# Shifting the low weight parts of a feed-forward by feature tile: 64, 192, 320 and 448 bytes in place of 64

## What is computed

```python
def swiglu(x, wi, wo):
    gate, up = jnp.split(x @ wi, 2, axis=-1)
    return (jax.nn.silu(gate) * up) @ wo
# per layer, D_MODEL = 1024, D_FF = 2816, SEQ = 256
h = h + 0.5 * swiglu(rmsnorm(h, ln_ffn1[i]), ffn1_wi[i], ffn1_wo[i])
h = h + mixer(rmsnorm(h, ln_mix[i]))
h = h + 0.5 * swiglu(rmsnorm(h, ln_ffn2[i]), ffn2_wi[i], ffn2_wo[i])
```

## Time and profile before

| | before |
|---|---|
| runs, median (lowest to highest) | 1936.55 us (1936.25 to 1936.56) |
| the profiled execution | 1937.1 us |
| its span, first to last instruction | 1935.4 us |
| PE busy | 1914.7 us, 99% of the span |
| PEld (weight loads) busy | 1653.1 us, 85% |
| DVE busy | 1366.3 us, 71% |
| ACT busy | 1128.9 us, 58% |
| chain that ended last, by engine | PE 93%, DVE 4%, ACT 2% |
| chain, by line | L698 33%, L535 31%, L706 17%, L993 5% |
| mean granted TensorE clock | 0.998 |

### The profile page before, as it was taken

The page is one execution under the profiler, slowest core; times in us unless marked ns, Lnnn a source line. Parts: engine busy times, 40 slices in busy tenths (PEclk is TensorE's granted clock), DMA queues, the critical chain, the costliest instruction groups (busy, mean ns, idle before and its releaser), DMA issues.

```text
span 1935.4 us, 29477 instructions
## 1 busy us (share of the span) xinstructions
PE 1914.7 (99%) x10740; PEld 1653.1 (85%) x10740; DVE 1366.3 (71%) x1844; ACT 1128.9 (58%) x1678; POOL 70.0 (4%) x151
## 2 busy tenths in 40 slices
PE   8999999999999999999999999999999999999998
PEld 6888988888888888888888889888888888978887
DVE  6766775777776697776776676676677777667666
ACT  6555575555655567655565555665555556656553
POOL 2000000000000002000010001000000000000000
PEclk9999999999999999999999999999999999999999
DMA  6556534655455554555655544355556555535553
GB/s 219 196 189 202 174 128 135 216 191 187 166 195 193 177 188 161 172 193 186 209 174 195 195 157 132 125 178 190 195 176 209 188 187 174 174 125 165 189 194 120
DMA packets 245264, 344.41 MB, mean 178 GB/s; under 512 B 12214, under 2 KB 197195, under 8 KB 245195
## 3 DMA queue, kind: packets, MB, share of 16 engines
q1 hardware_dynamic: 242016, 340.29, 53.2%
q10 hardware_dynamic: 3178, 3.18, 0.6%
HBM read 341.32 MB, written 1.06 MB: 177 GB/s over the span
## 4 chain that ended last, share of the span: by engine, by line
PE 93%; DVE 4%; ACT 2%; issue 0%; DMA 0%; SPq 0%; ACTq 0%; POOL 0%; POOLq 0%; DVEq 0%
PE psum L698 33%; PE psum L535 31%; PE psum L706 17%; PE psum L993 5%; DVE wlo L497 1%; PE psum L1644 1%; PE psum L566 1%; PE psum L1035 1%; DVE mix L1459 1%; ACT whi L478 1%; PE psum L1701 0%; DVE mix L1184 0%; DMA raw<-in_ffn_wi 0%; PE psum L1046 0%; PE psum L1731 0%
## 5 line engine op out<-in xcount | busy, mean ns | idle before, releaser
L478 ACT ACTIVATE whi<-raw,gains 128x512 fp32r<-128x512 f32 (+2 forms) x876 | 557.1, 709 | 260.6 <-PE psum L706 195.6
L698 PE MATMUL psum<-xT,whi 128*128 128x512 f32 x2816 | 679.4, 393 | 1.9 <-DVE wlo L518 1.5
L497 DVE SCALAR_TENSOR_TENSOR wlo<-raw,gains,whi 128x512 fp32r<-128x512 f32 (+2 forms) x876 | 596.0, 742 | 55.7 <-ACT whi L478 55.7
L698 PEld LDWEIGHTS psum<-xT,whi 128*128 128x128 f32 x2816 | 522.8, 188 | 111.1 <-issue 4.4
L706 PEld LDWEIGHTS psum<-xT,wlo 128*128 128x128 f32 x2816 | 344.4, 189 | 6.8
L706 PE MATMUL psum<-xT,wlo 128*128 128x256 f32 x2816 | 346.4, 281 | 0.0
L814 DVE TENSOR_TENSOR gate_in_T<-psum,low 128x512 f32<-128x512 f32 x88 | 60.8, 691 | 337.1 <-ACT low L761 336.7
L493 DVE TENSOR_TENSOR wlo<-raw,whi 128x2048 fp32r<-128x2048 f32 x100 | 228.5, 2285 | 43.4 <-ACT whi L474 43.4
L535 PE MATMUL psum<-whi,hidT_hi 128*128 128x512 f32 x640 | 249.0, 389 | 0.0
L535 PE MATMUL psum<-wlo,hidT_hi 128*128 128x512 f32 x640 | 249.0, 389 | 0.0
L535 PE MATMUL psum<-whi,hidT_lo 128*128 128x512 f32 x640 | 249.0, 389 | 0.0
(11 more groups left out here) (224 smaller groups left out, 1528.8 us busy)
## 6 DMA issues: line engine op xcount, KB each, us to landing
raw<-in_ffn_wi SPq DMA_DIRECT2D x350, 512.0 KB, 4.6
raw<-in_ffn_wo SPq DMA_DIRECT2D x176, 512.0 KB, 4.4
raw<-in_sb_w_in SPq DMA_DIRECT2D x48, 512.0 KB, 4.6
raw<-in_ml_w_in SPq DMA_DIRECT2D x24, 512.0 KB, 4.5
raw<-in_sb_w_out SPq DMA_DIRECT2D x16, 512.0 KB, 4.1
raw<-in_ml_w_out SPq DMA_DIRECT2D x8, 512.0 KB, 4.2
raw<-in_mla_w_out SPq DMA_DIRECT2D x8, 512.0 KB, 4.0
raw<-in_mla_w_in SPq DMA_DIRECT2D x4, 512.0 KB, 4.2
```

What stands on the lines that cost most here:

```text
L478: last = act.activation(whi[:, slot, r], raw[:, slot, r], ACT.Copy, scale=gain_col(p.gain + k))
L497: last = dve.scalar_tensor_tensor(wlo[:, slot, p.at + r.start:p.at + r.stop], raw[:, slot, r], gain_col(p.gain + k), hi[:, r], op0=ALU.mul ...
L698: i = pe.matmul(psum[:, 4 + blk, :], whi[:, slot, k * 2 * FC + blk * P:k * 2 * FC + (blk + 1) * P], xT[:, 4 * part + k, :, :].rearrange("p ...
```

## The change

The low part of feature tile k of an up piece is placed 16 + 32 k columns behind where its high part stands in the slot, in place of 16 for all four: 64, 192, 320 and 448 bytes. VectorE's writes (L497, and L518 for the first piece) and TensorE's weight loads (L706) use the new places. The number of instructions, their shapes, the waits, the transfers and all other pieces stay as they are; the last column written is 16 + 96 + 2048 = 2160 of 2176.

```diff
-SHIFT = 16
+SHIFT, STEP = 16, 32
...
-    def __init__(self, tiles, cols, gain, sources, views=None, at=0):
+    def __init__(self, tiles, cols, gain, sources, views=None, at=0, step=0):
         self.tiles, self.cols, self.gain, self.sources, self.views = tiles, cols, gain, sources, views
-        self.at = at
+        self.at, self.step = at, step
...
-                  for s in range(2)], at=SHIFT)
+                  for s in range(2)], at=SHIFT, step=STEP)
...
-                last = dve.scalar_tensor_tensor(wlo[:, slot, p.at + r.start:p.at + r.stop], raw[:, slot, r],
+                last = dve.scalar_tensor_tensor(wlo[:, slot, p.at + k * p.step + r.start:p.at + k * p.step + r.stop], raw[:, slot, r],
                                                 gain_col(p.gain + k), hi[:, r],
...
-                i = pe.matmul(psum[:, 4 + blk, 0:SEQ], wlo[:, slot, SHIFT + k * 2 * FC + blk * P:SHIFT + k * 2 * FC + (blk + 1) * P],
+                i = pe.matmul(psum[:, 4 + blk, 0:SEQ], wlo[:, slot, SHIFT + k * (2 * FC + STEP) + blk * P:SHIFT + k * (2 * FC + STEP) + (blk + 1) * P],
                               xT_hi[:, 4 * part + k, :], start=False, stop=False, skip_group_check=True)
```

More of the change, by code:

```diff
@@ L517, in first_dve @@
                 r = slice(k * p.cols, (k + 1) * p.cols)
-                dve.scalar_tensor_tensor(wlo[:, 0, p.at + r.start:p.at + r.stop], raw[:, 0, r], gain_col(p.gain + k),
+                dve.scalar_tensor_tensor(wlo[:, 0, p.at + k * p.step + r.start:p.at + k * p.step + r.stop], raw[:, 0, r],
+                                         gain_col(p.gain + k),
                                          whi[:, 0, r].bitcast(F32),
```

## The result

| | before | after |
|---|---|---|
| runs, median (lowest to highest) | 1936.43 us (1936.25 to 1936.56) | 1924.36 us (1924.32 to 1924.97) |
| the profiled execution | 1937.1 us | 1924.97 us |
| its span | 1935.4 us | 1923.2 us |
| PE busy | 1914.7 us | 1901.9 us |
| DVE busy | 1366.3 us | 1366.2 us |

The kernel before has a fourth run here, so its median is 1936.43 us. The changed kernel is faster by 12.1 us: the ratio is 0.9938, with a 95% interval of 0.9922 to 0.9954. The case that came is the rival "a gain: the steady 113 ns state", nearly in full (priced at 1923.8).

The account below looks back on a forecast made before the run. TensorE was taken as the bound, with only L706's matmul spacing counting in the feed-forwards. VectorE's writes at 0 us and L706's + 0.8 us on the median of 1936.55 gave about 1937.3 us, range 1927.0 to 1945.5.

Parts of the forecast that it names:

- a gain: the steady 113 ns state: Rival: L706's matmuls enter the 113 ns spacing seen at L1678; 1923.8 us in full, 1930.2 for half; chance 0.26.
- What bounds the kernel: TensorE, busy 99% of the span; in the feed-forwards L706's gain or loss goes straight into the time.
- What L706 costs, and what 1 ns is worth: L706: 117.7 ns start to start, 2727 distances, 321 us; 1 ns on each is worth 2.73 us.
- VectorE's writes cost nothing: The 704 instructions writing the up weights' low parts keep their length wherever they write, or are covered: 0 us.
- The spacing taken, 118.0 ns: L706's new start-to-start distance, 0.3 ns above the present one, over 2727 distances: + 0.8 us.
- two estimates: L706's new spacing: 116.8 ns as a mean over the four distances; 119.5 ns, or down to 117.2, from L1608's stepping.
- Against the gain: 45 matmuls at 192 ... never reach it: Argument against the 113 ns state: L1644's 45 matmuls at distance 192 run at 117.8 ns.
- The stepping of L1608 as the nearest analogue: L1608 steps through 0, 128, 256, 384 at every third matmul, averaging 119.5 ns; used to price L706's stepping.
- The correction that I offered for it, 2.3 ns: L1608 passes through distance 0, 2.3 ns dearer than 64, so its 119.5 ns could mean down to 117.2 for L706.
- The lower bound, 113.0 ns everywhere: All L706 distances at the lowest steady value seen: - 4.7 ns x 2727 = - 12.8 us.
- half of the gain and a bit more: Where the forecast range was cut on the fast side, 1927 us, leaving 10% out at each end.
- The rule of the Trainium skill: TensorE's separate read ports for weights and moving operand never wait, so L706's weight place is indifferent: 0 us, 1936.6.

Follow-up runs that it names:

- e2: Kernel before with all low parts of the up weights at a constant 448 bytes, no step, in place of 64: 1939.1 us.
- e6: Changed kernel with the feature tile as outer and the block as inner loop, so the distance steps only at every fourth low-part matmul: 1928.2 us.
- e7: Changed kernel with the low parts 64, 128, 192 and 256 bytes off by feature tile: 1933.2 us.
- e5: Changed kernel with the feature tiles taken in the order 3, 2, 1, 0 in the low parts' matmuls, a backward step: 1928.4 us.
- e10: Changed kernel with the low parts 64, 192, 192 and 192 bytes off by feature tile: 1928.2 us.
- e3: Changed kernel without the first 64 bytes of shift, low parts 0, 128, 256 and 384 bytes off: 1936.8 us.
- e9: Changed kernel with tokens moved 64 bytes against all weights; low parts keep their four distances, other distances, 0 before, become 448 or 64: 1955.0 us.
- e4: Kernel before with the up weights' high parts at 64, 192, 320 and 448 bytes and their low parts at 0: 1951.2 us.

## Why the prediction was wrong

- What bounds the kernel: right. 99% PE before and after, and a saving on L706 went into the time in full: 11.4 us less in the 88 runs, 12.1 us less in the time.
- What L706 costs, and what 1 ns is worth: right. (117.7 - 113.5) x 2727 = 11.5 us.
- VectorE's writes cost nothing: right, 745 ns each after as before.
- The spacing taken, 118.0 ns: wrong, it is 113.5. This is the term that failed, and with it the order of the cases. It came from two estimates, and both rested on the view that a distance or a step has a price, to be averaged or added. The runs show that the spacing depends on the sequence and on how it is entered: at a constant distance of 448 both 117.7 (e2) and 113.3 (e6) hold. A mean over distances says nothing about such a thing. For the change as it was made the run settled at 113.1 ns from the third matmul on. Other sequences do end between: e7 stays in a pattern of 116.8, and e5, e6 and e10 average 114.5 to 115.2 because they take 8 to 11 matmuls to settle.
- "Against the gain: 45 matmuls at 192 ... never reach it": a misreading by too narrow a window. I had one pass of L1644. A few microseconds later the kernel before runs the same line, at the same distances, in the short spacing. Timeline of PE, before:

```profile
1199.06 0.28 PE L1644 MATMUL psum<-sp_lo,whi 128*128 128x256 f32 x1
...
1200.08 0.28 PE L1644 MATMUL psum<-sp_lo,whi 128*128 128x256 f32 x1
```

  That is nine matmuls in 1.02 us, 113.3 ns each. Together with the passes of the earlier trace rows it was there to be read: two lines, two distances, and both values at each. There is also a fourth pass of L1678, which the prediction didn't count, in the short spacing, nine matmuls in 1.02 us, so it was three of four and not two of three:

```profile
1220.77 0.28 PE L1678 MATMUL psum<-whi,sp_lo 128*128 128x256 f32 x1
...
1221.79 0.28 PE L1678 MATMUL psum<-whi,sp_lo 128*128 128x256 f32 x1
```

  The prediction did say of L1678 that "what went before decides between them", and then went on to average the three passes.
- The stepping of L1608 as the nearest analogue (119.5 ns): wrong as a bound for this change. Its step is the same, but it passes through distance 0, and e3 shows what that does: with 0, 128, 256, 384 the feed-forward's matmuls stay at 118.1 ns. The correction that I offered for it, 2.3 ns, took distance 0 for a price per matmul, when it keeps the whole sequence out of the short spacing.
- The lower bound, 113.0 ns everywhere, - 12.8 us: right, and the result lies at it. The range was cut at 1927.0 as "half of the gain and a bit more", which is three quarters of it. So the gain in nearly its full size, the case that came, lay outside the range.
- The rule of the Trainium skill: by the Trainium skill, "SBUF — State Buffer", section "Who interferes with whom", TensorE never waits for another engine and its two read ports are independent; by that rule nothing would have changed. The measurement decides: 12.1 us hang on the place of the weights alone. That the two reads meet somewhere is the natural reading, but no run here shows where, so it stays a supposition.

What stays open: why 128 bytes from 64 leads in at once, why 64-byte steps never settle, and what it is in the hand-over from the 512-column matmuls that decides how long it takes. The runs describe this (three matmuls forward, eleven backward, eight with one pair of steps) and don't explain it. A step doesn't always lead in either: in the kernel before, L1644's matmuls at 113.3 ns up to 1200.08 are followed directly by L1678's, where the distance goes from 192 to 320, and these run at 118.0 ns, while the same step after L1644's 117.8 ns leads to 113.0.

## What to carry to other kernels

In a stretch where TensorE is the bound and loads new weights for every matmul, the place of the weights against the moving operand can be worth some per cent of the matmul at no cost in work (here 117.7 to 113.5 ns); read the spacing from start to start over whole runs and try a few offsets, with a step between neighbours, since a constant offset tells only half. When a trace shows one form of instruction at two spacings with the same distance, look for every pass of that form and don't average them: ask what leads into the better one, and let the range of the forecast reach the whole of either. A run may also settle in neither, as e7 does, or only after a third of its matmuls. Move only the operands of the form that gains, because here the 512-column matmuls lost 4 to 6 ns by the move that helped the 256-column ones.

## What the runs showed of the hardware

All at the granted clock of 0.997 to 0.998 of 2.4 GHz, 128x128 float32r weights loaded for each matmul:

- 256 moving columns: 119.4 to 120.0 ns at a constant distance of 0 modulo 512 bytes; 117.7 at a constant 64, 192 or 448 when entered from 512-column matmuls; 113.3 in the other state, also over four matmuls at one distance, be it 64, 192, 320 or 448 (e6), once it has been entered. Some sequences of distances settle in neither but repeat a pattern: 116.8 on average in e7, 118.5 in e3, 120 in 40 of the 87 runs of e9.
- 512 moving columns: of the places tried, shortest at distance 0. At 448 they are recorded 4 ns longer, at 64 (the down projection in e9) 6 ns longer, with the stepped high parts of e4 4 ns longer.
- The end of a run counts for the next: at a constant 192 or 448 the 16 matmuls of 512 columns behind it take 3.84 us, at 64 3.81 us; by the starts the difference is about 0.02 us.
